# Hybrid decoder layer on one core: first output product inside the mixing stage, exponentials one turn earlier, third token tile's gates by indirect adding DMAs

## What is computed

```python
y = jnp.concatenate([y_attn, y_rwkv], axis=-1) @ w_out[l]
x = _layer_norm(alpha * x + gt1 * y, ln1_g[l], ln1_b[l])
h = x * (1.0 + sc2) + sh2
# _peer(h, ...): 8 heads, 128 keys on each of two axes, 16 experts of each head and token
q = (hf @ wq).reshape(T, PEER_HEADS, 2, PEER_HALF)
s = jnp.einsum('thcd,hcnd->thcn', q, subkeys)
sv, si = lax.top_k(s, PEER_TOPK)
cand = sv[:, :, 0, :, None] + sv[:, :, 1, None, :]
fv, fpos = lax.top_k(cand.reshape(T, PEER_HEADS, PEER_TOPK * PEER_TOPK), PEER_TOPK)
fidx = jnp.take_along_axis(cidx..., fpos, axis=-1)          # cidx = i * 128 + j
gates = jax.nn.softmax(fv, axis=-1)
u = jnp.take(U, ic, axis=0);  act = gelu(jnp.einsum('chkd,cd->chk', u, xc))
vv = jnp.take(V, ic, axis=0); y = jnp.einsum('chk,chkd->cd', gc * act, vv)
x = _layer_norm(alpha * x + gt2 * y, ln2_g[l], ln2_b[l])
```

## Time and profile before

| | |
|---|---|
| median of 3 runs | 1939.82 us (1939.74 to 1940.1) |
| the profiled execution | 1939.86 us, of which 1938.1 us are the span in the trace |
| PE busy | 1834.6 us, 95% of the span |
| PEld / DVE / ACT / POOL busy | 84% / 75% / 39% / 30% |
| granted TensorE clock, mean | 0.983 |
| HBM read, written | 379.77 MB, 54.53 MB |

### The profile page before, as it was taken

One profiled execution on the slowest core, in us unless ns is written; L12 is line 12 of the kernel. 1 busy time (PEld: TensorE's weight loads), 2 busy tenths in 40 slices (PEclk: granted clock), 3 DMA queues, 4 the chain that ended last, 5 costly groups with the idle time before them and its releaser, 6 DMA issues.

```text
span 1938.1 us, 32958 instructions
## 1 busy us (share of the span) xinstructions
PE 1834.6 (95%) x10454; PEld 1622.7 (84%) x10454; DVE 1452.6 (75%) x2936; ACT 752.7 (39%) x1331; POOL 587.3 (30%) x446
## 2 busy tenths in 40 slices
PE   3999799997979999999999999999999999999996
PEld 3677688884479999989999999999988888888885
DVE  6786556563838787848888888877688888888887
ACT  2342433450144545544343444433343333333331
POOL 5013422230033444452223233235233333333310
PEclk9999999998989999999999999999999999999998
DMA  8741000005323433357998888899899999999981
GB/s 310 256 140 33 1 1 1 2 1 204 135 91 111 135 111 126 128 185 241 308 312 293 289 291 289 297 329 392 334 415 374 355 351 356 353 354 354 352 295 70
DMA packets 245052, 435.06 MB, mean 224 GB/s; under 512 B 84899, under 2 KB 157957, under 8 KB 244997
## 3 DMA queue, kind: packets, MB, share of 16 engines
q1 hardware_dynamic: 208132, 300.12, 44.8%
q0 software_dynamic: 36864, 134.23, 18.9%
HBM read 379.77 MB, written 54.53 MB: 224 GB/s over the span
## 4 chain that ended last, share of the span: by engine, by line
PE 68%; DVE 1%; DMA 1%; issue 1%; ACT 0%; POOL 0%; DVEq 0%; ACTq 0%; another core or an unknown queue 0%
PE bank L1559 26%; PE bank L1966 9%; PE bank L1967 9%; PE bank L1968 9%; PE bank L1539 6%; PE bank L1903 5%; PE bank L1949 4%; PE bank L1915 1%; DMA uraw<-in_peer_u,picks 0%; DMA vsel<-in_peer_v,picks 0%; POOL wide L1617 0%; DVE n_stats L1324 0%; DVE wide L2278 0%; DVE wide L2276 0%; DVE wide L1333 0%
## 5 line engine op out<-in xcount | busy, mean ns | idle before, releaser
L1559 PE MATMUL bank<-hh,uh 128*128 128x384 f32 x1024 | 358.0, 350 | 0.0
L1559 PE MATMUL bank<-hl,uh 128*128 128x384 f32 x1024 | 343.9, 336 | 0.0
L1966 PE MATMUL bank<-vh,wh 128*128 128x512 f32 x768 | 299.6, 390 | 3.1 <-DVE wl L2237 3.1
L1967 PE MATMUL bank<-vl,wh 128*128 128x512 f32 x768 | 299.4, 390 | 0.0
L1968 PE MATMUL bank<-vh,wl 128*128 128x512 f32 x768 | 299.3, 390 | 0.0
L1617 POOL DMA_INDIRECT vsel<-in_peer_v,picks x128 | 150.6, 1177 | 408.1 <-DVE gt L1643 393.8
L2070 ACT ACTIVATE vh<-vraw 128x1024 fp32r<-128x1024 f32 x128 | 135.9, 1062 | 287.3 <-PE bank L1968 273.5
L1617 POOL DMA_INDIRECT wide<-in_peer_u,picks x108 | 148.8, 1378 | 246.3 <-DVE wide L1624 232.4
L2234 DVE TENSOR_TENSOR vl<-vraw,vh 128x1024 fp32r<-128x1024 f32 x128 | 156.6, 1223 | 82.0 <-ACT vh L2070 82.0
L1559 PE MATMUL bank<-hh,ul 128*128 128x384 f32 x1024 | 198.9, 335 | 0.0
L1559 PEld LDWEIGHTS bank<-hl,uh 128*128 128x128 f32 x1024 | 193.6, 189 | 0.0
(11 more groups left out here) (342 smaller groups left out, 3229.4 us busy)
## 6 DMA issues: line engine op xcount, KB each, us to landing
urows<-in_peer_u SPq DMA_DIRECT2D x128, 512.0 KB, 5.6
vraw<-in_peer_v SPq DMA_DIRECT2D x128, 512.0 KB
scored<-act_out SPq DMA_DIRECT2D x128, 192.0 KB
gates<-SS SPq DMA_DIRECT2D x16, 1536.0 KB
gtile<-gates SPq DMA_DIRECT2D x32, 768.0 KB
act_in<-scored SPq DMA_DIRECT2D x128, 192.0 KB
wt<-in_w_in SPq DMA_DIRECT2D x19, 512.0 KB
wq<-in_peer_wq SPq DMA_DIRECT2D x18, 512.0 KB, 3.9
```

The costliest lines, as they stand in the source:

```text
L1559: last = pe.matmul(bank, u[:, k, :], h[:, k, 0:TD], start=(n == 0), stop=(n == 3 * KD - 1))
L1966: pe.matmul(b, wh[s][:, cols], vh[s][:, half], start=first, stop=False)
L1967: pe.matmul(b, wh[s][:, cols], vl[s][:, half], start=False, stop=False)
```

## The change

Three things are changed; the experts' base load is as it was.

1. **First output product in the mixing.** The 16 products of tile 0 (`output_rows(..., 0, None)`) are issued by PE at the end of the mixing block, behind `variances(3)`. In the output block PE only signals them (`pe.sem_inc(y_up, 2)`).
2. **Exponentials between the settling turns.** ACT takes the exponentials at the start of turn 9, and not after it; DVE's division (`gate_up`) follows it there.
3. **Third tile's gates by adding DMAs.** The one-hot spread covers tiles 0 and 1 alone (TH = 256 tokens): 16 tokens in a turn, 4 steps, one for each s, two slots. For tile 2 POOL issues 128 indirect DMAs, one for each head and pick, each of which adds 128 single gates (one 4-byte element for each token) to `added` in HBM at (i * 128 + j) * 128 + token. `added` (8.4 MB) is cleared by 8 DMAs from a zero tile at the start of the mixing. DVE computes the `places` before `ysel` is zeroed. The adding DMAs stand in POOL's order: 2 after each of s = 1, 2, 3 of turn 9, then in each spread turn 3 behind the U fetches and 4 behind the V fetches, then 4, 4 and 2 in turns 26 to 28. At the first of each head POOL waits until all 16 of the head before have landed. In the second pass each group's gates are two loads (512 KB of `gates`, 256 KB of `added`) and two multiplications on DVE; `load_gates(0, 0)` stands behind the last store of turn 30, after a wait for all adding DMAs.

```diff
@@ emit_mixing
+            flat = added.rearrange("i j t -> (i j t)").rearrange("(p m x) -> p m x", p=P, x=P)
+            for j in range(8):
+                sp.dma_start(flat[:, 16 * j:16 * j + 16, :], vtok[:, 0:1, :].broadcast_to([P, 16, P]))\
+                    .then_inc(cleared, 16)
...
             variances(NT - 1)
+            now, before = waits(pe, NT - 1)
+            now("stc", 2)
+            pe.wait_ge(wo_in, START + 16 * KD)
+            pe.wait_ge(ev["gn"], START + 1)
+            output_rows(pe, banks, yT, wo, 0, None)
...
+def output_rows(pe, banks, yT, wo, t, up):
+    for h in range(2):
+        for k in range(KD):
+            last = pe.matmul(banks[2 * (t % 2) + h][:, :], yT[:, k, t * P:(t + 1) * P],
+                             wo[k][:, 512 * h:512 * h + 512], start=(k == 0), stop=(k == KD - 1))
+        if up is not None:
+            last.then_inc(up, 1)
@@ emit_experts, steps and slots
-            return ((0, 1), (2,), (3, 4), (5,))[s]
+            return (s,)
-        SLOTS = 3
+        SLOTS = 2
@@ sync
             def load_gates(q, g):
                 sp.dma_start(gt[q][:, :, :, :].rearrange("p b j t -> p (b j t)"),
                              gates[:, bass.ds(g, 1), :, :].rearrange("p o b n -> p (o b n)")).then_inc(g_in[q], 16)
+                sp.dma_start(ga[q][:, :, :], added[:, bass.ds(4 * g, 4), :]).then_inc(g_in[q], 16)
...
-            load_gates(0, 0)
             for s in range(4):
                 experts(LAST - 1, s)
...
             scores.store(sp, LAST - 1, 3)
+            for h in range(HEADS):
+                sp.wait_ge(put[h], 16 * TOPK)
+            load_gates(0, 0)
             load_gates(1, 1)
@@ gpsimd
+            def put_gates(n):
+                for at in islice(picks_of, n):
+                    h, k = divmod(at, TOPK)
+                    if h and k == 0:
+                        pool.wait_ge(put[h - 1], 16 * TOPK)
+                    pool.indirect_dma_start(out=grid, out_offset=bass.IndirectOffsetOnAxis(
+                        ap=places[:, at:at + 1], axis=0), in_=FV[:, NT - 2, h, k:k + 1], in_offset=None,
+                        compute_op=ALU.add).then_inc(put[h], 16)
@@ scalar
-            with act.Fori(ROUTED, SPREAD) as i:
+            for i in range(ROUTED, SPREAD):
                 for s in range(4):
+                    if i == SPREAD - 1 and s == 0:
+                        act.wait_ge(less_up, START + 1)
+                        act.activation(FV[:, :, :, :], FV[:, :, :, :], ACT.Exp).then_inc(exp_up, 1)
                     following(i, s, False)
                     scores.gelu(act, i, s)
-            act.wait_ge(less_up, START + 1)
-            act.activation(FV[:, :, :, :], FV[:, :, :, :], ACT.Exp).then_inc(exp_up, 1)
@@ vector
-                dve.tensor_tensor(w[s % 2][:, :].rearrange("p (b t) -> p b t", t=TB),
-                                  act_in[:, s, :].rearrange("p (b t) -> p b t", t=TB), gt[q][:, :, s, :],
-                                  ALU.mult).then_inc(w_up, 1)
+                dve.tensor_tensor(w[s % 2][:, 0:TH].rearrange("p (b t) -> p b t", t=TB),
+                                  act_in[:, s, 0:TH].rearrange("p (b t) -> p b t", t=TB), gt[q][:, :, s, :],
+                                  ALU.mult)
+                dve.tensor_tensor(w[s % 2][:, TH:TD], act_in[:, s, TH:TD], ga[q][:, s, :], ALU.mult).then_inc(w_up, 1)
```

74 lines of the change are left out of this document (49 added, 25 removed).

## The result

| | before | after |
|---|---|---|
| median | 1939.8 us (6 runs beside the changed kernel) | 1924.11 us (6 runs, 1920.71 to 1930.68) |
| ratio, 95% interval | | 0.9922 (0.9902 to 0.9941) |
| profiled execution / span | 1939.86 / 1938.1 us | 1922.31 / 1920.6 us |

The change makes the kernel faster by 0.8%, 15.7 us. The forecast was 1909.2 us, a gain of 30.6 us; half of that is missing. The time lies within the range of 1896 to 1935 us.

A forecast was written before the change was run, and what follows sets the result against it. PE was taken to bound the spread turns, with the DMA engines having least room. 28.7 + 5.5 + 4.4 - 1.0 - 7.0 = 30.6 us off 1939.86 us gave 1909.2 us; range 1896 to 1935 us.

The forecast's parts named there:

- the POOL paragraph: Spread turns: seven more issues of 1.32 us fit POOL's turn of 23.81 us; waits at heads up to some 10 us.
- rival (c): Spread turns: POOL becomes late, DVE waits for rows, PE for DVE; some 1941 us, waits alone 1930 us; chance 0.08.
- rival (a): Spread turns: dear adding elements make DMA engines the bound; 2012 us at 170 ns (0.15 for 89+), some 1925 us (0.10).
- 32 fewer spread steps: Spread turns: 4 of 6 steps remain in 16 turns, 0.90 us of PE each, 28.7 us gained.
- output product: Mixing to output block: tile 0's product runs while PE idled; 5.5 us gained, between 3 and 10.0.
- exponentials: After turn 9: PE goes on sooner with gates ready; 4.4 us gained, up to 2 more if the clock stays up.
- turn 9: Turn 9: ACT's exponentials and table loads exceed its idle time ahead of a gelu; PE loses 1.0 us (0 to 3).
- late gates: Start of second pass: first gates, asked for later behind SP's queue, land 12 us after; 7.0 us lost, between 0 and 10.
- adding DMAs: Spread turns: seven a turn of 128 elements fit beside other DMA and POOL work; nothing booked.
- DVE's wait for the pieces: Output block: first `gate_sum` pieces land at 498.8 us, DVE wants them at 494.3 and waits 4.5 us.
- The DMA paragraph: Spread turns: an adding element costs 25 to 49 ns, 23.0 to 24.4 us a turn, just fits; PE waits above 55 ns.
- The rule of the Trainium skill: Adding DMAs: some 2.0 us fixed per GpSimd DMA, 14 us a turn if engine time; in series 2084 us, chance 0.02.

The follow-up runs named there:

- the regrouped adds: Changed kernel with its adds in groups of 3 or 4, so row fetches lie between one head's last add and the next head's first: 1920.65 us.
- moved back: Changed kernel with SP's wait for the adds and the first gate tiles' loads put back ahead of turn 30's loads: 1919.35 us.
- part 1 alone: Kernel before with only tile 0's output product moved to the end of the mixing's PE program: 1934.10 us against 1940.68.
- the rows fetched ahead: Changed kernel with turn 10's six rows fetched in turn 9, first gates loaded early, and adds grouped ahead of row fetches: 1912.09 us.
- the same two: POOL's two waits at first use of the fourth U and V row slots left out: changed kernel 1919.41 us; kernel before 1947.24 us.

## Why the forecast was off

**The step that failed** is the POOL paragraph: "Seven more issues of 1.32 us are 9.2 us on top of the 7.6 us in a turn of 23.81: it fits", with nothing booked. Three things in it were wrong.

1. *The price.* The 1.32 us were those of a row fetch. An adding DMA took 1.67 us, and each DMA needs 0.3 us ahead of it. That gap stands in the earlier trace rows (4.6 us of "issue" before 44 fetches: some 15 gaps of 0.3 us, the other fetches waiting for DVE instead), and it counts for 13 DMAs when POOL is full: 7 x 1.97 + 6 x 1.44 = 22.4 us of 23.8.
2. *The waits at the heads.* "Up to some 10 us, 7 times" was written down and then not added. They were 23.9 us in 385, that is 1.5 us a turn: 22.4 + 1.5 = 23.9 us, just above the turn. With that POOL has no slack, and what a delay takes beyond the lead of a fetch passes on to DVE and PE: steps were lost up to 969 us, and again from turn 26 on.
3. *The ends of the stretch.* "POOL's two adds after a low part fit between two low parts" is right for PE (turn 9 lost nothing), but it was not asked what else stood behind them: the first rows of turn 10. And at turn 26 stood a wait of POOL, harmless while POOL was 30% busy, that takes 9 us from a full one (4.0 + 5.4) and 16 us or more once POOL arrives there in time.

The mechanism is rival (c), POOL late, which had a chance of 0.08. Its figure for the waits alone, "7 of 3 us, 1930 us", is near the result only by luck: the waits were 3.4 us on average, but taking nearly all of them away gained 3.5 us and not 21 (the regrouped adds). The "some 1925 us" of rival (a) is nearer still, with the wrong resource. The time lies within the range, which was made wide for these rivals; the forecast's own sum, and its narrower range of 1901 to 1919 us, missed it.

**Point by point**, forecast and measured:

| term | forecast | shown by |
|---|---|---|
| 32 fewer spread steps | 28.7 | 64 x 5.94 against 32 x 12.80 us: 29.4 |
| output product | 5.5 | alone 6.6; in the changed kernel the experts' first transposes come 5.7 us sooner |
| exponentials | 4.4 | alone 7.6; in its trace 4.2 at the gap and some 2 behind it, where the clock had been low |
| turn 9 | -1.0 | no loss in the trace |
| late gates | -7.0 | -4.8 (moved back); gap in the trace 5.66 |
| adding DMAs | 0 | -17.4 (left out) |

The output block ended as told: its start at 472.93 us (forecast 472.05), DVE's wait for the pieces 3.41 us (4.5), ended at 498.71 (498.8). One wait in it was not foreseen: with tile 0's product ready at once, DVE waits 6.28 us for the residual `xs`, whose load starts only with the block. It cost nothing, since the product that DVE needed next, tile 1's, ended only at 486.90 us. The start is late because the mixing ended 1.2 us later than before (its last `variances` at 455.64 in place of 454.48 us); with part 1 alone, without the clearing of `added`, they stand at 454.89 us. So the clearing, booked at nothing, cost less than 1 us if anything:

```profile
456.50 13.90 PE L1372 MATMUL bank<-PK,wide 128*128 128x512 f32 x32
472.93 13.97 PE L1372 MATMUL bank<-PK,wide 128*128 128x512 f32 x32 [2.53 <-PEq L1405]
```
```profile
480.48 1.23 DVE L1483 SCALAR_TENSOR_TENSOR x<-xs,x 128x1024 f32<-128x1024 f32 x1 [6.28 <-DMA xs<-in_x]
498.71 0.49 DVE L1499 TENSOR_SCALAR act_out<-vsel,par 128x512 f32<-128x512 f32 x1 [3.41 <-DMA vsel<-in_ada_w]
```

Of the exponentials, "up to 2 more if the shorter gap keeps the clock up" was the likelier case and stood only as an upper end. Of the late gates, 11 us from request to landing were forecast as 12. The right column adds up to 21.4 us, and 15.7 were measured. The single parts were timed on other chips and each with an error of some 2 us or more. In the two profiled executions the terms close better. The experts start 5.7 us sooner (543.12 and 537.39 us), turn 10 starts a further 3.8 us sooner, and from there to the last transposes of the first pass PE needs 515.4 in place of 524.0 us, 8.7 less. That is about 29.4 for the steps, less some 18 of stalls and 5.8 at the gates, plus some 3 us of longer steps that the kernel before had there (2.3 of them behind its low clock at turn 10). The three savings together are 18.3 us, and the spans differ by 17.5.

Whether the gates' gap costs more than its length is open. In the kernel without adds PE needed 540.3 us from its last transposes to its end, 4.5 more than the 535.8 before, with the granted clock at 0.84 from 1350 to 1370 us. The changed kernel had a clock of 0.83 from 1360 to 1380 us, and there that stretch took 535.7 us.

**The DMA paragraph held.** An element costs what was taken: q0's share of the spread turns rose from 37.8% without adds to 46.3% for 16261 more packets, 0.085 x 16 x 385 us / 16261 = 32 ns (forecast 25 to 49, threshold 55). With the rows fetched ahead the engines read 0.99 and PE was busy for 385.00 of 385 us. Rival (a), which had a quarter of the chances, had the wrong resource: the scarce one was the engine that issues. The rule of the Trainium skill that stood against the change (DMA: Bandwidth & Descriptors, Anatomy of one DMA: some 2.0 us fixed for every DMA issued by GpSimd) is near in size to what POOL itself spent on an add, 1.97 us by the rows above, but that is a coincidence: the page puts most of it down to the receipt of the write, and a row fetch took POOL 1.44 us. I had asked whether it is in series for the DMA engines, and not what a DMA costs POOL in series.

## What to carry to other kernels

Price an instruction that an engine issues by its own duration plus the gap ahead of it, multiply by all that the engine issues in the period, and add its waits: here an engine that was busy for 30% of its time was full with 7 x 2 us more in 24 us, since the gaps and waits, which no busy share shows, count too. A queue without slack turns every late start and every spare wait in its order into lost time, so look at both ends of the stretch, put what is needed first ahead of what can wait, and put other work between an operation and the wait for its landing. A wait that looks spare may have a use: leaving out the same two gained 4.7 us in one kernel and lost 7.7 us in the other, so time its removal by itself.

## What the hardware showed beyond that

- POOL needs about the same time for an indirect adding DMA of 2 elements (1498 ns) as for one of 128 (1670 ns), with 0.3 us ahead of each when it is not waiting.
- An element of 4 bytes added in HBM took 32 ns of a DMA engine in the spread turns, a little more than a small packet that is only written (25 to 29 ns).
- The last add of a head landed 6.29 and 7.76 us after the start of its issue. POOL's waits for such landings were no shorter with 2 elements in each DMA (28.5 us in 385) than with 128 (23.9 us), and nearly vanished (2.5 us) where row fetches stood between an add and the wait for it.
- A stream of POOL subtractions on SBUF operands doubled DVE's 128x128 comparisons from 367 to 733 ns over a whole stretch; indirect DMAs issued by POOL did not (367 ns with the adds, 352 without).
